# Expert stages of a two-block transformer: four of sixteen value rows added by VectorE, the dot product written over its own row, semaphores counted in groups of four

## The reference

```python
q = (xt @ w_pq).reshape(T, PEER_HEADS, 2, PEER_QDIM // 2)
s = jnp.einsum('thpd,hpnd->thpn', q, subkeys)
top_s, top_i = lax.top_k(s, PEER_TOPK)            # two lists of 16 a head
...                                               # the best 16 of their 256 sums: expert, gate = softmax
act = jax.nn.gelu(jnp.einsum('thkd,td->thk', peer_u[eb], xb)) * gb
return jnp.einsum('thk,thkd->td', act, peer_v[eb])
```

## Time and profile before

| | |
|---|---|
| three timed runs | 1970.73, 1973.23 (median), 1973.85 us |
| profiled execution, span | 2142.0 us, 22067 instructions |
| profiled execution, its own time around the span | the page doesn't give it |
| first stages, to 405 us | PE busy 378 us |
| first expert stage, 405 to 1164 us | 512 gathers |
| second block, 1164 to 1372 us | PE busy 196 us |
| second expert stage, 1372 to 2142 us | 512 gathers |

### The profile page before, as it was taken

How to read it: one execution, slowest core, us unless ns; L and a number is a source line. 1 busy time by engine, 2 the same in 40 slices (tenths; PEclk the granted TensorE clock), 3 DMA queues, 4 the chain that set the end, 5 groups by cost and what they waited for, 6 DMA issues and landing times. The chain is left out here.

```text
span 2142.0 us, 22067 instructions
## 1 busy us (share of the span) xinstructions
PE 1722.3 (80%) x7643; PEld 1082.0 (51%) x7643; DVE 1254.5 (59%) x2789; ACT 616.9 (29%) x1151; POOL 1008.5 (47%) x1095
## 2 busy tenths in 40 slices
PE   8999999978787686768668999877777867677768
PEld 7998898844443232323224999754442322222323
DVE  6544665885565665566453456685555566476553
ACT  4472644412121111222213455312212111212212
POOL 3021000366666666667672000265666666666663
PEclk9998999989998787878778999898997878788878
DMA  7521553999999999999997756598999999999996
GB/s 253 165 82 60 172 188 116 307 365 341 347 371 373 351 367 383 352 366 368 361 391 241 232 161 197 187 338 332 342 367 375 361 364 370 365 372 370 359 376 240
DMA packets 243719, 644.22 MB, mean 301 GB/s; under 512 B 19541, under 2 KB 105354, under 8 KB 243610
## 3 DMA queue, kind: packets, MB, share of 16 engines
q0 software_dynamic: 147456, 536.94, 66.3%
q1 hardware_dynamic: 96154, 105.88, 15.4%
HBM read 641.69 MB, written 1.05 MB: 300 GB/s over the span
## 5 line engine op out<-in xcount | busy, mean ns | idle before, releaser
L2038 DVE SCALAR_TENSOR_TENSOR ex_uj<-wring,ps 128x1024 f32<-128x1024 f32 x496 | 601.8, 1219 | 409.7 <-DMA wring<-in_peer_u,ex_idx 363.7
L2334 PE MATMUL ps<-ex_v,ex_diag 128*128 128x512 f32 x1328 | 664.6, 647 | 168.4 <-issue 162.6
L2196 POOL DMA_INDIRECT wring<-in_peer_u,ex_idx x496 | 468.6, 945 | 176.1 <-issue 141.4
L2334 PEld LDWEIGHTS ps<-ex_v,ex_diag 128*128 128x128 f32 x1328 | 270.6, 206 | 546.2 <-issue 535.0
L2334 PE MATMUL ps<-value_rows,ex_diag 128*128 128x512 f32 x664 | 360.0, 677 | 135.4 <-issue 134.0
L2211 POOL DMA_INDIRECT ex_v<-in_peer_v,ex_idx x336 | 318.1, 947 | 242.3 <-remote 110.8
L2162 ACT ACTIVATE ex_diag<-ident,ex_weight 128x128 f32<-128x128 f32 x500 | 171.0, 393 | 720.0 <-remote 390.1
L2334 PEld LDWEIGHTS ps<-value_rows,ex_diag 128*128 128x128 f32 x664 | 141.7, 215 | 351.0 <-issue 345.4
L208 DVE TENSOR_TENSOR w_lo<-wring,w_hi 128x1024 fp32r<-128x1024 f32 (+1 forms) x160 | 187.3, 1211 | 108.4 <-ACT w_hi L199 106.1
L2196 POOL DMA_INDIRECT ex_v<-in_peer_u,ex_idx x16 | 16.4, 1023 | 464.1 <-PE ps L283 459.9
L2211 POOL DMA_INDIRECT value_rows<-in_peer_v,ex_idx x172 | 164.2, 955 | 96.3 <-remote 47.2
(11 more groups left out here) (470 smaller groups left out, 2465.0 us busy)
## 6 DMA issues: line engine op xcount, KB each, us to landing
wring<-in_w_in SPq DMA_DIRECT2D x42, 1024.0 KB, 5.4
wring<-in_w_ckv SPq DMA_DIRECT2D x8, 1024.0 KB, 5.3
wring<-in_peer_u,ex_idx POOLq DMA_INDIRECT x496
ex_v<-in_peer_v,ex_idx POOLq DMA_INDIRECT x336
wring<-in_w_mix_out SPq DMA_DIRECT2D x4, 1024.0 KB, 6.6
wring<-in_w_cq SPq DMA_DIRECT2D x4, 1024.0 KB, 5.1
wring<-in_w_co SPq DMA_DIRECT2D x4, 1024.0 KB, 5.2
value_rows<-in_w_pq SPq DMA_DIRECT2D x4, 1024.0 KB, 10.3
```

What stands on the lines that cost most here:

```text
L2038: ve.scalar_tensor_tensor(out=uj[i % 2], in0=u_row(i), scalar=1.0, in1=tokens(g // PH), op0=ALU.mult, op1=ALU.mult, accum_out=hidden[:, g ...
L2196: nc.gpsimd.indirect_dma_start(u_row(i), None, table_u, bass.IndirectOffsetOnAxis(ap=idx[:, g // PH, i % PER_T:i % PER_T + 1], axis=0)).th ...
L2334: last = mm(ps[:, 2 * T + c, :], diag[:, n % DIAGS, :], value_slot(v_slot(j))[:, c * BANK:(c + 1) * BANK], start=j % PER_T == 0, stop=ends)
```

## The change

In each group but the last, VectorE adds four of the 16 value rows itself (rows 2, 6, 10 and 14 of the group), as it did six in the last. It does so in the next group, behind dot products 1, 3, 7 and 11 (`VEC_ROWS`). TensorE and ScalarE have no product and no diagonal for them. The dot product writes its product over the up-row it has read, `uj` is gone, and so is the wait for the dot product before last. Diagonals and products are counted in groups of four (`DIAG_GROUP`): one increment for four, and one wait for four. GpSimd waits, for a slot whose last row was VectorE's, on `vec_used` instead of `pe_used`. The order of the gathers is as it was.

```diff
-DIAGS = 12
+DIAGS, DIAG_GROUP = 12, 4
+VEC_ROWS = {1: 2, 3: 6, 7: 10, 11: 14}
...
         def on_vector(j):
-            return j >= FIRST_LAST and j - FIRST_LAST in LAST_VEC
+            return j - FIRST_LAST in LAST_VEC if j >= FIRST_LAST else j % TOPK in VEC_ROWS.values()
+
+        def before_on_vector(j):
+            return sum(1 for i in range(j) if on_vector(i))
...
+        def value_row(v, j):
+
+            T, g = j // PER_T, j // TOPK
+            v_arrived(v, j)
+            n = before_on_vector(j)
+            if n:
+                v.wait_ge(vec_used.sem, vec_used.at(n))
+            nc.vector.scalar_tensor_tensor(out=K.X[:, T, :], in0=value_slot(v_slot(j)), scalar=weight[:, g % 2, j % TOPK:j % TOPK + 1],
+                                           in1=K.X[:, T, :], op0=ALU.mult, op1=ALU.add).then_inc(vec_used.sem, 1)
+
+        def group(j):
+            return on_tensor(j) // DIAG_GROUP
+
+        def groups(j):
+            return -(-on_tensor(j) // DIAG_GROUP)
+
+        def ends_group(n):
+            return n % DIAG_GROUP == DIAG_GROUP - 1 or n == TENSOR_ROWS - 1
...
                     u_arrived(v, i)
-                    if i >= 2:
-                        v.wait_ge(u_used.sem, u_used.at(i - 1))
                     if i % PER_T == 0:
                         v.wait_ge(x_ps.sem, x_ps.at(g // PH + 1))
-                    ve.scalar_tensor_tensor(out=uj[i % 2], in0=u_row(i), scalar=1.0, in1=tokens(g // PH),
+                    ve.scalar_tensor_tensor(out=u_row(i), in0=u_row(i), scalar=1.0, in1=tokens(g // PH),
                                             op0=ALU.mult, op1=ALU.mult, accum_out=hidden[:, g % 2, s:s + 1]).then_inc(u_used.sem, 1)
+                    if g and s in VEC_ROWS:
+                        if s == min(VEC_ROWS):
+                            v.wait_ge(wts.sem, wts.at(g))
+                        value_row(v, (g - 1) * TOPK + VEC_ROWS[s])
                     if s == 0 and g:
                         weigh(g - 1)
...
-                    if n >= DIAGS:
-                        act.wait_ge(pe_used.sem, pe_used.at(n - DIAGS + 1))
-                    nc.scalar.activation(diag[:, n % DIAGS, :], K.ident[:, :], ACT.Copy,
-                                         scale=weight[:, g % 2, s:s + 1]).then_inc(dia.sem, 1)
+                    if n >= DIAGS and n % DIAG_GROUP == 0:
+                        act.wait_ge(pe_used.sem, pe_used.at((n - DIAGS) // DIAG_GROUP + 1))
+                    made = nc.scalar.activation(diag[:, n % DIAGS, :], K.ident[:, :], ACT.Copy,
+                                                scale=weight[:, g % 2, s:s + 1])
+                    if ends_group(n):
+                        made.then_inc(dia.sem, 1)
...
                 elif v_use(j):
-                    pool.wait_ge(pe_used.sem, pe_used.at(max(m for m in range(j) if slots[m] == n) + 1))
+                    m = max(m for m in range(j) if slots[m] == n)
+                    if on_vector(m):
+                        pool.wait_ge(vec_used.sem, vec_used.at(before_on_vector(m) + 1))
+                    else:
+                        pool.wait_ge(pe_used.sem, pe_used.at(group(m) + 1))
...
-                pe.wait_ge(dia.sem, dia.at(n + 1))
+                if n % DIAG_GROUP == 0:
+                    pe.wait_ge(dia.sem, dia.at(group(j) + 1))
                 v_arrived(pe, j)
...
-                last.then_inc(pe_used.sem, 1)
+                if ends_group(n):
+                    last.then_inc(pe_used.sem, 1)
```

More of the change, by code:

```diff
@@ L1718, in stage_peer @@
         first_row = 2 * K.query_slot
-        uj = sb("uj", [P, D])[:, :], sb("uj", [P, D])[:, :]
         tss, tsd, tiv = (sb(n, [P, NT * after]) for n in ("tss", "tsd", "tiv"))
@@ L1847, in _ @@
                     if n == RAW - 1:
-                        sp.wait_ge(pe_used.sem, pe_used.at(ROWS - len(LAST_VEC)))
-                        sp.wait_ge(vec_used.sem, vec_used.at(len(LAST_VEC)))
+                        sp.wait_ge(pe_used.sem, pe_used.at(groups(ROWS)))
+                        sp.wait_ge(vec_used.sem, vec_used.at(VECTOR_ROWS))
                     K.load_unit(sp)
@@ L1992, in weigh @@
                 if g >= 2:
-                    v.wait_ge(dia.sem, dia.at(TOPK * (g - 1)))
+                    v.wait_ge(dia.sem, dia.at(groups(TOPK * (g - 1))))
                 v.wait_ge(g_inv.sem, g_inv.at(g + 1))
@@ L1999, in add_tokens @@
             def add_tokens(T):
-                v.wait_ge(pe_used.sem, pe_used.at(on_tensor(PER_T * (T + 1))))
+                v.wait_ge(pe_used.sem, pe_used.at(groups(PER_T * (T + 1))))
                 ve.tensor_tensor(K.X[:, T, :], K.X[:, T, :], ps[:, 2 * T:2 * T + 2, :].rearrange("p b c -> p (b c)"),
@@ L2057, in _ @@
                     first_low(n - len(LAST_VEC) + 3)
[L2058 to L2063, removed]
+                value_row(v, j)
+            v.wait_ge(vec_used.sem, vec_used.at(VECTOR_ROWS))
             add_tokens(NT - 1)
@@ L2169, in _ @@
             if unit:
-                act.wait_ge(pe_used.sem, pe_used.at(on_tensor(more_tensor) + 1))
-                act.wait_ge(vec_used.sem, vec_used.at(LAST_VEC.index(more_vector - FIRST_LAST) + 1))
+                act.wait_ge(pe_used.sem, pe_used.at(group(more_tensor) + 1))
+                act.wait_ge(vec_used.sem, vec_used.at(before_on_vector(more_vector) + 1))
                 for half in range(2):
@@ L2331, in _ @@
                     pe.wait_ge(s_out.sem, s_out.at(QSTEPS))
-                ends = j == PER_T - 1 or n == ROWS - len(LAST_VEC) - 1
+                ends = j == PER_T - 1 or n == TENSOR_ROWS - 1
                 for c in range(2):
@@ L2340, in _ @@
                 first_product()
-        for sig, by in ((tk, TK_EARLY + TK_STEPS * HEADS), (picked, HEADS + 1), (u_used, ROWS), (pe_used, ROWS - len(LAST_VEC)),
-                        (vec_used, len(LAST_VEC)), (dia, ROWS - len(LAST_VEC)), (out_r, NT), (x_ps, NT), (g_exp, HEADS), (g_inv, HEADS),
+        for sig, by in ((tk, TK_EARLY + TK_STEPS * HEADS), (picked, HEADS + 1), (u_used, ROWS), (pe_used, groups(ROWS)),
+                        (vec_used, VECTOR_ROWS), (dia, groups(ROWS)), (out_r, NT), (x_ps, NT), (g_exp, HEADS), (g_inv, HEADS),
                         (act_r, HEADS), (wts, HEADS), (ready, HEADS),
```

4 lines of the change are left out of this document (3 added, 1 removed).

## The result

The changed kernel takes 2033.21 us (median of four runs, 2028.49 to 2034.25) against 1971.98 for the kernel before (four runs, 1966.92 to 1973.85): ratio 1.0318, 95% interval 1.0297 to 1.0339. It is slower by 61 us; the forecast was 26.

What follows compares the result with a forecast made beforehand. In timed runs GpSimd was taken to issue gathers nearly back to back, close to the DMA limit, with TensorE having time to spare. Terms: 22 (held gathers) + 4 (last group) = +26 us, 1999 us; range 1940 to 2041.

Steps and rivals of the forecast that it cites:

- Writing the dot product over its row, and counting in groups of four: Expert stages: removed waits were long done, slots counted up to 5 us late had 25 us to spare; price nothing.
- The choice of the 169 us: Profiled span exceeds timed median by 169 us; mostly slow-MATMUL stretches absent from timed runs, leaving some 44 us of waits.
- TensorE's relief: Four rows in 16 leave TensorE, 6.9 us less a group; worth nothing in a timed run, hidden under 39.8 us of gathers.
- They hold up GpSimd: VectorE's two-SBUF-input instructions lengthen gathers in the expert stages: 120 × 0.43 = 52 us of GpSimd, bounds nothing to 125.
- The term of 22 us: Held gathers not hidden under DMA: 1.7 us a group less 1.0 hidden, 0.7 us in 30 groups.
- The last group: End of each expert stage: VectorE waits for value rows 234 and 238, last weights come later; 2 us a stage, 4 in all.
- GpSimd alone as the bound: Rival: unprofiled transfers beat 411 GB/s, so no held gather hides; +52 + 4, 2029 us; chance 0.16.
- The signs to look for: Trace after: gathers lengthened, mean 0.95 to 1.0 us; slot waits well under 200; TensorE about 210 less; span 2060 to 2120.

Runs made afterwards that it cites:

- f2: Changed kernel with diagonals and products counted by the row, on a chip where the kernel before takes 1969.18 us: 1973.87 us, 1.0018.
- k1: Changed kernel with products counted by the row, diagonals still in fours, where the kernel before takes about 1970 us: 1981.2 us, 1.0055.
- k2: Changed kernel with diagonals counted by the row, products still in fours, where the kernel before takes about 1970 us: 2027.43 us, 1.0279.
- f4: Kernel before, dot product written over its row, plus 120 unused VectorE instructions with two SBUF inputs; before takes 1969.18 us: 1969.44 us, 1.0003.
- e1: Changed kernel with diagonals and products counted by the row, on a chip where the kernel before takes 2128.05 us: 2119.41 us, 0.9955.
- e4: Kernel before with only the dot product written over its row, on a chip where before takes 2128.05 us: 2130.54 us, 1.0009.
- g1: Changed kernel with products counted by the row, diagonals in fours, on a chip of the long kind: 2135.48 us, 0.9976.
- h3: Changed kernel with everything counted by the row and group 14's rows back on TensorE, on a chip of the long kind: 2125.32 us, 0.9987.
- m1: Changed kernel with everything counted by the row and group 14's rows back on TensorE, where before takes about 1970 us: 1967.76 us, 0.999.
- f3: Changed kernel with the four late queries moved to the starts of fours, where the kernel before takes 1969.18 us: 1996.9 us, 1.0136.
- e2: Changed kernel without VectorE's four value rows, counting in fours kept, on a chip where before takes 2128.05 us: 2141.12 us, 1.0062.
- g4: Kernel before, dot product written over its row, plus 120 unused VectorE instructions with one input in PSUM, long kind of chip: 2140.27 us, single run.

## Why the prediction was wrong

It had the direction, and a time within its range; the sum was wrong by 35 us, and the range held by luck, since the mechanism that cost the time was priced at nothing. Point by point:

- **The step that failed: "Writing the dot product over its row, and counting in groups of four … Nothing, in either".** The two fours cost 56 us, nearly the whole change (f2): some 50 for the products', 7 for the diagonals' (k1 and k2). The argument said "A slot is asked for again 20 value rows, 50 us, after its gather" and "25 are left". 20 is the number of slots; in the first 68 rows of a stage the list of slots goes round 12 to 14. Six rows less are 15 us of the 25; at row 46 some 7 were left, from 1459 to 1465.8. The step also took "up to three rows, 5 us" for the delay, and overlooked that a query stands inside the four: from row 32's end to its count, near 1472.5, it is 13 us. Both were in the code and in the trace of before. The other edit of that step, the dot product over its row, is worth nothing, as forecast (it is in f4, 1.0003).
- **The choice of the 169 us was wrong.** They are no product of recording. On some chips timed runs are as long as profiled spans, at 2104 us and more (e1 to e4, g1 to h3); on the others both are short (f2: 1973.1 and 1973.87). That the earlier trace rows show the same pauses as e1 is the natural reading, and not shown. (Rows 7 give the clock as a mean of 0.63 over 12 us; the 0.50 that the prediction reads there is in finer windows of the same trace, from 1718 us on.) The conclusion drawn from it, that timed runs of 1973 us are free of them, was nevertheless right.
- **TensorE's relief is worth nothing where the kernel takes 1970 us.** Right: it has 182 us less to do (1618.6 in f4, 1436.7 in f2; 210 were forecast), and the time isn't shorter. On the other kind of chip it is worth little: e1 has 8.6 us less than before, 0.9955, with 242 us less of TensorE's work than e4.
- **"They hold up GpSimd": right in kind, and the size depends on the chip.** The 0.43 us an instruction were read from 12 instructions in a trace of the long kind, and on that kind 120 of them do cost 0.44 each (e1 against e4). On the short kind, where the change was timed, it is about 0.27: the changed kernel's (1040.9 - 1008.5) / 120, with the 1008.5 from a trace of the long kind. Why the kinds differ here is open. The forecast hid 1.0 us a group under the DMA engines. 4 × 0.27 = 1.1 us, so next to nothing of it should stick out, and f4 measures 1.0003. The term of 22 us measured 0.3, with 3 to either side.
- **The last group** was put at 4 us and measured 5.5, give or take 4 (m1 against f2, on two chips): right in size. Of its mechanism, 2 us a stage behind the last gather, the second stage shows about 2; but 4.0 us lie ahead of the last gathers, where the prediction had nothing.
- **The rivals.** GpSimd alone as the bound would have given 2029, near the measured 2033, by another mechanism, which f4 excludes: the held gathers cost nothing. DMA at 409 or 410 GB/s is the bound once the waits are gone.
- **The signs to look for** came in part. The gathers are lengthened, with means of 0.97 to 0.99. The span was to be 2060 to 2120 and is 2032.5. Slot waits "well under 200 us" held and misled: the 62.8 us of them are the loss.

Of the 61 us, then: 56 for the fours, the diagonals' 7 among them, and 5 for the last group. Within the fours, 33 go with the place of the queries (f3). The other 23 are, by the waits of f3, mostly the same lateness without a query, about half of it at the stage's first four. Why the diagonals' fours cost 7 us is not shown. Whether fours would cost anything with all 16 rows on TensorE is open too: e2 was timed only where the pauses cover it. Also open is why some chips pause; nothing in the records of the engines says it. m1 is the best version made, at 0.999 with an interval that holds 1: with 1.276 us a gather, 512 gathers need 653 us a stage, and m1 takes 657.9 and 659.1 from the first gather to the last. There is little left to win by this road.

## What to carry to other kernels

Before counting a buffer's release in groups, find the tightest reuse of any buffer in the group, not the mean and not the ring's size, and add all work that the releasing engine has between the first member and the last. The time at which a count comes is that of the last member with everything queued before it. And where a bound by DMA bandwidth stands 2 or 3% above the issuing engine, as here, costs on that engine are free up to it, and relief elsewhere is worth nothing.

## What was not expected of the hardware

- Gathers of 128 rows of 4 KB run at 407 to 411 GB/s over hundreds of us, 1.276 us for 0.524 MB. By the Trainium skill (SBUF — State Buffer, "SBUF: two separate sides") about 436 GB/s is the most that DMA can move into SBUF; no stretch shown here has more than 412.
- The same kernel takes 1970 us on some chips and 2128 to 2140 on others. The latter pause several times a stage: in the pause shown, DMA falls from 410 to 147 GB/s. TensorE's granted clock is 0.50 there, its level of 1.2 GHz, after it had stood still.
- A VectorE instruction of 128x1024 with two SBUF inputs lengthens a gather's issue by 0.44 us on average on chips of the long kind (e1 against e4), by about 0.27 on the others, and at most by 1.05 (1.99 us at 687.73 in the changed kernel, against 0.94); the same with one input in PSUM doesn't (g4). The Trainium skill has it so (SBUF — State Buffer, "Who interferes with whom"): a VectorE instruction with two SBUF inputs contends with a GpSimd instruction that reads SBUF; one with at most one, outside the modes that use two ports, does not. The runs agree: 149 and 127 lengthened gathers in f4 and e1, against 40 in g4.
